# A decoder block on one core: x and the normed x turned by VectorE instead of TensorE in the front

## The chip, the core and the metric

The kernel runs on one core of one Trainium2 chip. The metric is the device time of one execution in microseconds, the median of several runs. TensorE's granted clock is 1.00 of its upper level in the part of the run that matters here.

## What is computed

One layer of a hybrid decoder block, 1024 tokens of width 1024, float32:

```
u   = RMSNorm(x)
P   = u @ W_in                     -> [B | C | h | q | k | v]
y_c = B * causal_dwconv3(C * h)
y_a = sliding-window attention (8 heads, 2 kv heads, window 128, QK-norm, ALiBi, sinks)
x   = x + concat(RMSNorm(y_c), RMSNorm(y_a)) @ W_out
xn  = RMSNorm(x)
x   = x + MoE(xn)                  (64 experts, top 8 of 4 groups, and one shared expert)
```

## The kernel before

Tokens lie in 8 tiles of 128 rows. The kernel has a front (the mixer, tile by tile, and the router's part of the MoE), a short middle in which the shared expert runs while the table of routed jobs is made, and a long stage of routed jobs. Each engine has its own program, written out by hand in order, and the engines meet only by semaphores. The front of every engine is the function `step(T, N, NN, B)`, called for T = tiles 0 to 6: T is the tile whose attention runs, N the next (its input projection runs), NN the one after (its x is made ready), B the one before (its residual, norm and routing run). Tile 7 (TL) has a tail of its own, and tile 6 (TB) is its B.

TensorE contracts over partitions, so every operand with tokens in partitions has to be turned before it is projected. Three things are turned in each step:

- `t_x(NN)` (L745): eight 128x128 transposes of x into PSUM `psT`. VectorE's `read_uT` (L1389) multiplies by the norm's weight and writes `uT`, of which there is one. `project` (L754) reads it. The scale 1/rms of a row is applied later, when ScalarE's `read_group` (L1111) copies a projected group out of PSUM.
- `t_xn(B)` (L833): eight transposes of the normed residual `xn` into `psT`. ScalarE's `read_xn` (L1182) copies them to `xnT`, which shares its memory with `yT`. `router` (L839) reads it, and SP stores it to DRAM.
- `t_y(T)` (L812): the mixer's output, likewise. It is not touched.

TensorE's step, in order: project(N, group 0), scores(T), project(N, 1), t_xn(B), project(N, 2), t_p(T) (turning the probabilities), part of project(N, 3), p_v(T), router(B), the rest of project(N, 3) and half of project(N, 4), t_y(T), the rest of project(N, 4), out_project(T, 0), t_qk(N), position(B), t_x(NN), out_project(T, 1).

VectorE's step, in order (L1602): x1_add(B) (residual add out of PSUM, L1512), xn_rms(B), xn_scale(B) (L1525), soft_a(T) (scores times scale plus bias, L1454), soft_b(T) (row maxima, L1465), u_mul(N) (C * h, L1397), conv(N) (L1401), o_norm(T) (L1477), y_attn_rms(T), route(B) (L1530), read_yT(T) (L1496), qk_norm(N), x_rms(NN), read_pos(B), read_uT(NN), conv_gate(N), slots(B), y_conv_rms(N).

What ties them: ScalarE's exps(T) wait for soft_b, t_p waits for the exps. On ScalarE read_group(N, 1), the h group, stands behind the exps, and u_mul waits for it. SP's `shift_u(N)` stores C * h to DRAM behind u_mul and reads it back shifted by one and by two rows; conv waits for that. o_norm scales p_v's result; ScalarE squares and scales y_attn, and t_y waits for both halves of y. read_yT(T) stands behind route(B) on VectorE, and out_project(T, 0) waits for it. x1_add waits for out_project(T, 1) of the step before. GpSimd computes the reciprocal roots, stores xn and the residual (`store`, L595), and then, from step 2 on, issues eight indirect DMAs (`scatter_slots`, L615). x is loaded by SP into one of three buffers `x_sb` (L388), which later holds the residual too; the load of NN waits for the store of B's residual.

In the routed stage VectorE turns the gathered rows with STREAM_TRANSPOSE (`turn_x`, L1645, 64 partitions x 512 elements, read with a step of 8 words) and the hidden activations (`turn_h`, L1667, 32 partitions x 64 elements, read in runs of 32 words). The instruction turns blocks of 32x32.

```
def t_xn(T):
    pe.wait_ge(s_xn_ready, (T.t + 1) * 3)
    for k in range(KT):
        i = nc.tensor.transpose(psT[:, k, :], xn.rearrange("t (p k) -> t k p", k=KT)[:, k], ident[:, :])
    i.then_inc(s_txn, 1)
```

Of the kernel before, what the change touches and what calls it, by code (L numbers as in the profile page):

```python
# [20 lines left out]
P = 128  # L21
# [5 lines left out]
class Tile:  # L27


    def __init__(self, t):  # L30
        self.t, self.par, self.buf, self.use = t, t % 2, (t + 1) % 3, t // 3 + 1
        self.rows = slice(t * P, (t + 1) * P)


def hymba_moe(nc, x, mix_norm_w, w_in, conv_w, q_norm_w, k_norm_w, sinks, conv_out_norm_w, attn_out_norm_w,
# [36 lines left out]
    with ExitStack() as ctx:  # L72
# [55 lines left out]
        x_sb = cut(3 * D).rearrange("p (b n) -> p b n", b=3)  # L128
# [3 lines left out]
        uT = cut(D).rearrange("p (k n) -> p k n", k=KT)  # L132
# [67 lines left out]
        xT_shared = [uT] + [area[:, o:o + D].rearrange("p (k n) -> p k n", k=KT) for o in (gates_at, gates_at + 2 * DC)] + \  # L200
# [103 lines left out]
        x_ld = [sem(f"x_ld{b}") for b in range(3)]  # L304
# [25 lines left out]
        TB, TL = tiles[-2:]  # L330

# [55 lines left out]
        def _(sp):  # L387
            def load_x(T):  # L388
                sp.dma_start(x_sb[:, T.buf], x2[T.rows, :]).then_inc(x_ld[T.buf], 16)
# [35 lines left out]
            def step(T, N, NN, B):  # L425
# [114 lines left out]
        def _(pool):  # L540
# [54 lines left out]
            def store(T):  # L595
# [5 lines left out]
                pool.dma_start(x1_dram[T.rows, :], x_sb[:, T.buf]).then_inc(x1_st[T.par], 16)  # L601
# [139 lines left out]
        def _(pe):  # L741
# [3 lines left out]
            def t_x(T):  # L745

                pe.wait_ge(x_ld[T.buf], T.use * 16)
                if T.t == 1:
                    pe.wait_ge(s_uT_ready, 1)
                for k in range(KT):  # L750
                    i = nc.tensor.transpose(psT[:, k, :], x_sb[:, T.buf, k * P:(k + 1) * P], ident[:, :])  # L751
                i.then_inc(s_tx, 1)

            def project(T, g, ks=range(KT)):  # L754
# [8 lines left out]
                for k in ks:  # L763
                    i = mm(psP[:, bank, 0:n], uT[:, k, :], w_in_sb[:, k, c0:c0 + n], k == 0, k == KT - 1)
# [47 lines left out]
            def t_y(T):  # L812
                pe.wait_ge(s_yc_scaled, T.t + 1)
                pe.wait_ge(s_ya_scaled, T.t + 1)
                if T.t:
                    pe.wait_ge(s_xnT_ready, T.t)
                else:
                    pe.wait_ge(s_uT_ready, 2)
# [33 lines left out]
            def step(T, N, NN, B):  # L852
# [14 lines left out]
                if B:  # L867
                    t_xn(B)
# [23 lines left out]
                if NN:  # L892
                    t_x(NN)
# [96 lines left out]
            t_x(tiles[0])  # L990
# [3 lines left out]
            t_x(tiles[1])  # L994
# [109 lines left out]
        def _(act):  # L1104
            A = nc.scalar.activation

            def x_square(T):
                act.wait_ge(x_ld[T.buf], T.use * 16)
                A(junk[:, :], x_sb[:, T.buf], ACT.Square, accum_out=st_x[:, 0:1]).then_inc(s_x_sq, 1)
# [68 lines left out]
            def x1_square(T):  # L1178
                act.wait_ge(s_x1_ready, T.t + 1)
                A(junk[:, :], x_sb[:, T.buf], ACT.Square, accum_out=st_n[:, 0:1]).then_inc(s_x1_sq, 1)  # L1180

            def read_xn(T):  # L1182
                act.wait_ge(s_txn, T.t + 1)
# [8 lines left out]
            def step(T, N, NN, B):  # L1192
# [12 lines left out]
                if B:  # L1205
                    read_xn(B)
# [137 lines left out]
        def _(dve):  # L1344
# [44 lines left out]
            def read_uT(T):  # L1389

                dve.wait_ge(s_tx, T.t + 1)
                if T.t:
                    dve.wait_ge(s_proj, T.t * NGR)
                V.tensor_tensor(uT, psT[:, :, :], bc(mixw[:, :].unsqueeze(2), [P, KT, P]), ALU.mult) \
                 .then_inc(s_uT_ready, 1)
# [120 lines left out]

            def xn_rms(T):

                dve.wait_ge(s_x1_sq, T.t + 1)
                if T.t:  # L1520
                    dve.wait_ge(s_txn, T.t)
# [360 lines left out]
```

## Time and profile before

| what | value |
|---|---|
| median of 3 runs | 1391.63 us (1389.9 to 1392.19) |
| the profiled execution | 1393.29 us, its span 1391.5 us |
| TensorE busy | 1364.0 us (98%) |
| VectorE busy | 942.7 us (68%) |
| ScalarE busy | 690.1 us (50%) |
| GpSimd busy | 562.7 us (40%) |
| the front (tiles 0 to 6 stepped) | 0 to 441.6 us |
| the middle | 441.6 to about 525 us |
| routed jobs and end | about 525 to 1391.5 us |

PE is TensorE, DVE VectorE, ACT ScalarE, POOL GpSimd, SP SyncE; L743 is the helper that issues every matmul. An instruction's row names what it writes and reads; `area` is the one large buffer in which most of the front's tiles lie, so rows are told apart by their line. "[5.53 <-PE ...]" at a row's end is the idle time of the engine before it and what ended it.

### The profile page before, as it was taken

To read this page: it belongs to the slowest core of one execution; us is meant where nothing else is said; L and a number is where in the kernel's file an instruction comes from. 1 tells how busy PE (TensorE), PEld (TensorE's weight loads), DVE (VectorE), ACT (ScalarE), POOL (GpSimd) and SP (SyncE) were. 2 spreads that over 40 slices of the span, in tenths; PEclk is the share of its full clock that TensorE was granted. 3 is DMA by queue.
4 is the path that set the end of the run, shared out by engine and by line. 5 is a ranking of instruction groups with operands and counts; after the bars stand their busy time and mean duration, and the time that the engine had idled before them with its cause. 6 is when DMAs were issued, how large, how long until landed. Compare 5 with 4: busy or idle time off the path is not lost.

```text
span 1391.5 us, 23960 instructions
## 1 busy us (share of the span) xinstructions
PE 1364.0 (98%) x5899; PEld 584.3 (42%) x5900; DVE 942.7 (68%) x2243; ACT 690.1 (50%) x646; POOL 562.7 (40%) x713
## 2 busy tenths in 40 slices
PE   7999999999999988999999999999999999999997
PEld 3456565565655542333333333333333333333333
DVE  2334443444535457888888888888888888888852
ACT  1223233233233311766666666666666666666640
POOL 3010303123031352555555555555555555555521
PEclk9999999999999999999999999999999999999999
DMA  9412112021116536999999999999999999999937
GB/s 343 188 61 84 46 38 84 13 72 46 38 69 283 190 123 222 347 355 315 354 332 379 322 322 356 288 300 276 318 317 375 368 350 329 332 321 299 373 49 215
DMA packets 76033, 330.10 MB, mean 237 GB/s; under 512 B 16008, under 2 KB 17545, under 8 KB 50325
## 3 DMA queue, kind: packets, MB, share of 16 engines
q1 hardware_dynamic: 45140, 249.62, 46.4%
q0 software_dynamic: 30848, 79.94, 23.3%
q8 instruction: 22, 0.36, 0.1%
q14 instruction: 23, 0.18, 0.0%
HBM read 282.74 MB, written 65.11 MB: 250 GB/s over the span
## 4 chain that ended last, share of the span: by engine, by line
PE 94%; DMA 3%; issue 1%; another core or an unknown queue 1%; ACT 0%; DVE 0%; SPq 0%; ACTq 0%; POOL 0%; POOLq 0%; DVEq 0%
PE psP L743 59%; PE psW L743 32%; DMA area<-x_dram 2%; PE psW L794 1%; DMA wts<-in_w_in_dram 1%; PE psT L820 1%; PE psT L836 1%; PE psT L751 0%; DMA area<-xn_dram,rows_i 0%; PE psW L771 0%; DVE bias L1651 0%; DMA x_dram<-area,sidx 0%; ACT wts L1261 0%; SPq L526 0%
## 5 line engine op out<-in xcount | busy, mean ns | idle before, releaser
L743 PE MATMUL psP<-wts,bias 128*64 (+1 forms) x1296 | 572.8, 595 | 7.9 <-DVE bias L1651 4.9
L743 PE MATMUL psP<-area,bias 128*64 128x512 f32 x1264 | 558.1, 594 | 0.0
L743 PE MATMUL psW<-wts,area 128*64 (+2 forms) x1592 | 426.6, 592 | 1.5 <-ACT wts L1261 0.9
L1651 DVE STREAM_TRANSPOSE bias<-area 64x512 f32<-64x512 f32 x316 | 352.3, 1115 | 8.1 <-DMA area<-xn_dram,rows_i 2.5
L743 PEld LDWEIGHTS psP<-wts,bias 128*64 128x64 f32 (+1 forms) x1296 | 179.4, 139 | 371.8 <-issue 371.8
L1672 DVE STREAM_TRANSPOSE area<-dsq 32x64 f32<-32x64 f32 x1264 | 298.4, 236 | 22.4
L743 PE MATMUL psP<-wts,area 128*128 128x512 f32 (+1 forms) x704 | 288.3, 561 | 5.6 <-DMA wts<-in_w_in_dram 4.3
L1268 ACT ACTIVATE area<-wts 128x4096 f32 x77 | 278.6, 3618 | 16.1 <-DMA wts<-in_w_exp_up_dram 6.6
L743 PEld LDWEIGHTS psW<-wts,area 128*64 128x64 f32 (+1 forms) x1592 | 153.1, 147 | 247.3 <-issue 245.8
L674 POOL DMA_INDIRECT area<-xn_dram,gidx x150 | 156.3, 1042 | 93.0 <-POOL gidx L670 65.3
L1251 ACT ACTIVATE area<-psW 128x1024 f32<-128x1024 f32 x79 | 80.9, 1024 | 226.9 <-PE psW L743 150.4
L743 PEld LDWEIGHTS psP<-wts,area 128*128 128x128 f32 x704 | 131.3, 192 | 136.7 <-issue 128.3
L698 POOL DMA_INDIRECT out_dram<-area,sidx x79 | 117.3, 1485 | 152.8 <-ACT area L1251 118.0
L743 PEld LDWEIGHTS psP<-area,bias 128*64 128x64 f32 x1264 | 173.6, 138 | 0.0
L1261 ACT ACTIVATE wts<-wts 128x2048 f32 x79 | 150.9, 1911 | 37.3 <-issue 35.6
L698 POOL DMA_INDIRECT x_dram<-area,sidx x79 | 112.5, 1424 | 25.4 <-issue 24.5
L1662 DVE SCALAR_TENSOR_TENSOR dsq<-dsq,area,psP 128x256 f32<-128x256 f32 x79 | 53.1, 672 | 84.8 <-ACT dsq L1235 82.8
L555 POOL TENSOR_TENSOR st_y<-st_y,minus_half 128x1 f32<-128x1 f32 x16 | 8.9, 557 | 180.7 <-DVE st_y L1349 180.7
L1132 ACT ACTIVATE area<-psP,st_x 128x512 f32<-128x512 f32 x32 | 21.8, 683 | 100.7 <-PE psP L743 95.8
L624 POOL DMA_INDIRECT slot_table<-pay,slot_i x64 | 62.6, 978 | 20.1 <-issue 19.1
L670 POOL COPY gidx<-rows_i 128x2 int32 x75 | 14.1, 188 | 123.5 <-DVE bias L1651 123.3
L1235 ACT ACTIVATE dsq<-psP 128x256 f32<-128x256 f32 x87 | 32.0, 368 | 55.2 <-PE psP L743 39.6
(225 smaller groups left out, 743.9 us busy)
## 6 DMA issues: line engine op xcount, KB each, us to landing
wts<-in_w_exp_gate_dram SPq DMA_DIRECT2D x64, 1024.0 KB
wts<-in_w_exp_up_dram SPq DMA_DIRECT2D x64, 1024.0 KB
wts<-in_w_exp_down_dram SPq DMA_DIRECT2D x64, 1024.0 KB
wts<-in_w_in_dram SPq DMA_DIRECT2D x4, 2048.0 KB, 17.4
area<-in_x_dram SPq DMA_DIRECT2D x8, 512.0 KB
wts<-in_w_out_dram SPq DMA_DIRECT2D x1, 4096.0 KB, 18.3
area<-u_dram SPq DMA_DIRECT2D x16, 256.0 KB, 2.9
xn_dram<-area POOLq DMA_DIRECT2D x16, 256.0 KB
```

The source lines that it names most:

```text
L624: pool.indirect_dma_start(out=table[:, :], out_offset=bass.IndirectOffsetOnAxis(ap=slot_i[:, n:n + 1], axis=0), in_=pay[:, t, j, :], in_of ...
L674: pool.indirect_dma_start(out=xg[:, par, g], out_offset=None, in_=xn_halves, in_offset=bass.IndirectOffsetOnAxis(ap=gidx[:, 2 * par + g:2 ...
L698: pool.indirect_dma_start(out=(out2, x1_dram)[b][:, :], out_offset=bass.IndirectOffsetOnAxis(ap=sidx[b][:, par:par + 1], axis=0), in_=ysb[ ...
L743: return nc.tensor.matmul(out_, lhsT, rhs, start=start, stop=stop)
L1132: A(dst, psP[:, bank, 0:n], ACT.Copy, scale=st_x[:, 2:3]).then_inc(s_proj_out, 1)
L1235: A(sg, psP[:, par, 0:FE], ACT.Silu).then_inc(s_silu, 1)
L1251: A(ysb[:, par], psW[:, 2:4, :].rearrange("p a n -> p (a n)"), ACT.Copy).then_inc(s_y_ready, 1)
L1261: A(dn_b, wts[:, bass.ds((e % NSLOT) * SLOTW + 2 * GUW, FT * D)], ACT.Copy).then_inc(s_dn_copy, 1)
L1268: A(gu_b[par].rearrange("p m k f -> p (m k f)"), wts[:, bass.ds((e % NSLOT) * SLOTW, 2 * GUW)], ACT.Copy) \
L1651: i = V.transpose(xT[par][u * HB:(u + 1) * HB, :, b * HB:(b + 1) * HB] .rearrange("p k (g t) -> p g k t", g=2), rows[:, u])
L1662: V.scalar_tensor_tensor(out=hh.rearrange("t (f p) -> t p f", f=FT), in0=sg.rearrange("t (p f) -> t p f", f=FT), scalar=w, in1=psP[:, par, ...
L1672: i = V.transpose(hT[1 - par][q * QUAD:(q + 1) * QUAD, :, t * QUAD:(t + 1) * QUAD], hh[t * QUAD:(t + 1) * QUAD].rearrange("t (f q p) -> t ...
```

## The change

x and the normed x are turned by VectorE, in 16 STREAM_TRANSPOSEs of 32 partitions x 256 elements each (`turn_x(NN)`, in two halves around u_mul; `turn_xn(B)`, behind xn_scale). x of tile 0 and the normed x of tiles 6 and 7 stay with TensorE. `turn_x` writes `uT` of the tile's parity, and `scale_uT` multiplies it in place. x comes into one buffer `x_in`; the residual has its own, `x_res`, loaded by a second DMA (tile 7's residual stays in `x_in`). ScalarE's read_xn goes from the step. The old `turn_x` of the routed stage is only renamed.

```diff
-        x_sb = cut(3 * D).rearrange("p (b n) -> p b n", b=3)
+        x_in, x_res = cut(D), cut(D)
+        uT_odd = cut(D).rearrange("p (k n) -> p k n", k=KT)
...
+        uT = [uT_even, uT_odd]
...
@@ SP
+            sp.wait_ge(s_tx, 1)
+            sp.wait_ge(s_x_sq, 1)
             load_x(tiles[1])
             sp.dma_start(w_out_sb, w_out[0].rearrange("(k p) n -> p k n", p=P)).then_inc(s_wout_ld, 16)
-            load_x(tiles[2])
+            load_residual(tiles[0])
...
-                if B and NN:
+                if NN:
+                    sp.wait_ge(s_tx, N.t + 1)
+                    sp.wait_ge(s_x_sq, N.t + 1)
+                    load_x(NN)
+                if B:
                     sp.wait_ge(x1_st[B.par], (B.t // 2 + 1) * 16)
                     sp.wait_ge(s_xn_ready, T.t * 3)
-                    load_x(NN)
+                    load_residual(T)
...
@@ TensorE, step
-                if B:
-                    t_xn(B)
...
-                if NN:
-                    t_x(NN)
...
-            t_x(tiles[1])
...
@@ ScalarE, step
-                if B:
-                    read_xn(B)
...
@@ VectorE
+            def turn_x(T, part=range(P // QUAD)):
+
+                if 0 in part:
+                    dve.wait_ge(s_x_ld, (T.t + 1) * 16)
+                    if T.t >= 2:
+                        dve.wait_ge(s_proj, (T.t - 1) * NGR)
+                for a in part:
+                    rows = x_in[a * QUAD:(a + 1) * QUAD].rearrange("t (k p) -> t k p", k=KT)
+                    for q in range(P // QUAD):
+                        i = V.transpose(uT[T.par][q * QUAD:(q + 1) * QUAD, :, a * QUAD:(a + 1) * QUAD],
+                                        rows[:, :, q * QUAD:(q + 1) * QUAD])
+                if P // QUAD - 1 in part:
+                    i.then_inc(s_tx, 1)
...
+            def turn_xn(T):
+                dve.wait_ge(s_xn_ready, T.t * 3 + 3)
+                for a in range(P // QUAD):
+                    rows = xn[a * QUAD:(a + 1) * QUAD].rearrange("t (p k) -> t k p", k=KT)
+                    for q in range(P // QUAD):
+                        i = V.transpose(xnT[q * QUAD:(q + 1) * QUAD, :, a * QUAD:(a + 1) * QUAD],
+                                        rows[:, :, q * QUAD:(q + 1) * QUAD])
+                i.then_inc(s_xnT_ready, 1)
...
                     xn_scale(B)
+                    turn_xn(B)
                 soft_a(T, first)
                 soft_b(T, first)
+                if NN:
+                    turn_x(NN, range(0, 2))
                 if N:
                     u_mul(N)
+                if NN:
+                    turn_x(NN, range(2, 4))
+                if N:
                     conv(N)
...
                 if NN:
-                    read_uT(NN)
+                    scale_uT(NN)
```

## Rows read from the trace of the kernel before

**Rows 1.** The page's chain that ended last, shares by engine.
```profile
PE 94%; DMA 3%; issue 1%; another core or an unknown queue 1%; ACT 0%; DVE 0%; SPq 0%; ACTq 0%; POOL 0%; POOLq 0%; DVEq 0%
```

**Rows 2.** The chain in time order, one step; columns: start us, us, what.
```profile
270.66 6.87 PE psP L743 x16
277.53 1.99 PE psW L743 x32
...
286.58 0.89 PE psT L836 x8
...
294.33 1.75 PE psW L794 x16
...
312.64 6.87 PE psW L743 x16
...
320.14 0.91 PE psT L751 x8
```

**Rows 3.** Busy time by stretch: PE, PEld, DVE, ACT, POOL, clock, DMA share, GB/s.
```profile
98.90:441.60 342.70, 342.70 (x1434) 199.08 (x1433) 153.02 (x370) 110.06 (x231) 76.22 (x87) 1.00 0.20 65
```

**Rows 4.** VectorE's groups by shape, whole run: busy us, mean ns, idle before.
```profile
L1651 DVE STREAM_TRANSPOSE bias<-area 64x512 f32<-64x512 f32 x316 | 352.3, 1115 | 8.1 <-DMA area<-xn_dram,rows_i 2.5
L1672 DVE STREAM_TRANSPOSE area<-dsq 32x64 f32<-32x64 f32 x1264 | 298.4, 236 | 22.4
L1662 DVE SCALAR_TENSOR_TENSOR dsq<-dsq,area,psP 128x256 f32<-128x256 f32 x79 | 53.1, 672 | 84.8 <-ACT dsq L1235 82.8 <-issue 1.8
...
L1380 DVE SCALAR_TENSOR_TENSOR bias<-area 128x256 f32<-128x256 f32 x8 | 2.8, 418 | 0.0
...
L1774 DVE TENSOR_SCALAR ring_i<-psW 128x102 int32<-128x102 f32 x1 | 0.3, 252 | 0.0
...
L1691 DVE CAST area<-psW 64x102 int32<-64x102 f32 x1 | 0.2, 245 | 0.0
```

**Rows 5.** The timeline of the same step, VectorE, and one row of ScalarE.
```profile
270.70 1.23 DVE L1514 TENSOR_TENSOR area<-psW,area 128x1024 f32<-128x1024 f32 x1 [2.60 <-PE psW L743]
...
273.96 1.28 DVE L1527 SCALAR_TENSOR_TENSOR area<-area,st_n,ffnw 128x1024 f32<-128x1024 f32 x1 [0.67 <-POOL st_n L555]
280.77 2.29 DVE L1460 SCALAR_TENSOR_TENSOR area<-psW,bias 128x2048 f32<-128x2048 f32 x1 [5.53 <-PE psW L743]
...
289.85 0.19 ACT L1147 ACTIVATE st_s<-st_s 128x8 f32<-128x8 f32 x1
290.65 0.69 DVE L1399 TENSOR_TENSOR area<-area 128x512 f32<-128x512 f32 x1 [4.78 <-ACT area L1132]
297.36 0.69 DVE L1406 TENSOR_TENSOR area<-area,convw 128x512 f32<-128x512 f32 x1 [6.02 <-DMA area<-u_dram]
...
302.27 0.69 DVE L1488 TENSOR_TENSOR area<-psW,st_s 128x512 f32<-128x512 f32 x1 [1.13 <-PE psW L743]
...
305.29 0.23 DVE L1542 TENSOR_TENSOR bi<-sc,rbias 128x64 f32<-128x64 f32 x1 [1.38 <-ACT sc L1190]
...
310.95 1.22 DVE L1501 TENSOR_TENSOR area<-psT,outw 128x1024 f32<-128x1024 f32 x1 [0.67 <-PE psT L820]
```

**Rows 6.** The timeline of GpSimd, same step: the third indirect DMA.
```profile
280.62 0.96 POOL L624 DMA_INDIRECT slot_table<-pay,slot_i  x1 [0.30 <-issue]
```

**Rows 7.** The timeline of the routed stage: a turn beside an indirect DMA.
```profile
803.62 4.51 DVE L1651 STREAM_TRANSPOSE bias<-area 64x512 f32<-64x512 f32 x4
803.70 1.49 POOL L698 DMA_INDIRECT out_dram<-area,sidx  x1 [1.66 <-ACT area L1251]
```

**Rows 8.** The timeline of the start and of step 0.
```profile
47.21 5.39 PE L743 MATMUL psP<-wts,area 128*128 128x512 f32 x12 [1.36 <-issue]
...
65.75 0.68 DVE L1399 TENSOR_TENSOR area<-area 128x512 f32<-128x512 f32 x1
...
76.89 0.69 DVE L1488 TENSOR_TENSOR area<-psW,st_s 128x512 f32<-128x512 f32 x1 [0.81 <-PE psW L743]
...
80.98 1.04 PE L820 MATMUL psT<-ident,area 128*128 128x128 f32 x8
```

More of the change, by code:

```diff
@@ L303, in hymba_moe @@
         s_x_sq = sem("x_sq")
-        x_ld = [sem(f"x_ld{b}") for b in range(3)]
+        s_x_ld = sem("x_ld")
+        s_res_ld = sem("res_ld")
         g_ld = [sem(f"g_ld{b}") for b in range(2)]
@@ L330, in hymba_moe, with residual @@
         TB, TL = tiles[-2:]
+        def residual(T):
+            return x_in if T is TL else x_res
         def side(j):
@@ L388, in load_x, with load_residual @@
             def load_x(T):
-                sp.dma_start(x_sb[:, T.buf], x2[T.rows, :]).then_inc(x_ld[T.buf], 16)
+                sp.dma_start(x_in, x2[T.rows, :]).then_inc(s_x_ld, 16)
+            def load_residual(T):
+                sp.dma_start(x_res, x2[T.rows, :]).then_inc(s_res_ld, 16)
             load_x(tiles[0])
@@ L600, in store @@
                                    xn.rearrange("t (u h n) -> t h u n", u=2, h=2)[:, h]).then_inc(s_xn_st, 16)
-                pool.dma_start(x1_dram[T.rows, :], x_sb[:, T.buf]).then_inc(x1_st[T.par], 16)
+                pool.dma_start(x1_dram[T.rows, :], residual(T)).then_inc(x1_st[T.par], 16)
             def rsqrt_qk(T):
@@ L743, in mm, with t_x_first @@
                 return nc.tensor.matmul(out_, lhsT, rhs, start=start, stop=stop)
[L745 to L749, printed above, removed]
+            def t_x_first():
+                pe.wait_ge(s_x_ld, 16)
                 for k in range(KT):
-                    i = nc.tensor.transpose(psT[:, k, :], x_sb[:, T.buf, k * P:(k + 1) * P], ident[:, :])
+                    i = nc.tensor.transpose(psT[:, k, :], x_in[:, k * P:(k + 1) * P], ident[:, :])
                 i.then_inc(s_tx, 1)
@@ L989, in _ @@
             pe.wait_ge(s_const_pool, 3)
-            t_x(tiles[0])
+            t_x_first()
             for g in range(NGR):
@@ L1520, in xn_rms @@
                 if T.t:
-                    dve.wait_ge(s_txn, T.t)
+                    if T is TL:
+                        dve.wait_ge(s_txn, 1)
+                    else:
+                        dve.wait_ge(s_xnT_ready, T.t)
                     dve.wait_ge(s_xn_st, T.t * 32)
@@ L1526, in xn_scale @@
                 dve.wait_ge(s_xn_ready, T.t * 3 + 2)
-                V.scalar_tensor_tensor(out=xn, in0=x_sb[:, T.buf], scalar=st_n[:, 2:3], in1=ffnw[:, :], op0=ALU.mult,
+                V.scalar_tensor_tensor(out=xn, in0=residual(T), scalar=st_n[:, 2:3], in1=ffnw[:, :], op0=ALU.mult,
                                        op1=ALU.mult).then_inc(s_xn_ready, 1)
+            def turn_xn(T):
[6 more added lines that the diff above has]
+                i.then_inc(s_xnT_ready, 1)
             def route(T):
@@ L1634, in _ @@
             dve.wait_ge(s_mixw_ld, 16)
-            read_uT(tiles[0])
+            scale_uT(tiles[0])
             constants()
             u_mul(tiles[0])
-            read_uT(tiles[1])
+            turn_x(tiles[1])
+            scale_uT(tiles[1])
             qk_norm(tiles[0])
@@ L1643, in _, with turn_rows @@
             y_conv_rms(tiles[0])
-            def turn_x(j, par, nth):
+            def turn_rows(j, par, nth):
                 dve.wait_ge(g_ld[par], nth * 32)
@@ L1801, in _ @@
             read_shared(2, side(2))
-            turn_x(NSH, 0, 1)
+            turn_rows(NSH, 0, 1)
             read_shared(3, side(3))
-            turn_x(NSH + 1, 1, 1)
+            turn_rows(NSH + 1, 1, 1)
             dve.wait_ge(s_xn_st, 32 * NT)
@@ L1809, in _ @@
             turn_h(NSH, 0)
-            turn_x(NSH + 2, 0, 2)
+            turn_rows(NSH + 2, 0, 2)
             h_mul(NSH + 1, 1, tab_w[:, 1:2])
             turn_h(NSH + 1, 1)
-            turn_x(NSH + 3, 1, 2)
+            turn_rows(NSH + 3, 1, 2)
             def jobs(i, ks):
@@ L1819, in jobs @@
                     turn_h(r + NSH, k)
-                    turn_x(r + (NSH + 2), k, i + 3)
+                    turn_rows(r + (NSH + 2), k, i + 3)
             one = routed_jobs(dve, 2, jobs)
```

41 lines of the change are left out of this document (20 added, 21 removed).

## The prediction

> **What bounds the kernel now.** I read the chain of waits first. It gives TensorE 94% of the span [rows 1]. That is an average over three stages, so the stage that the edit touches has to be read by itself: the front, eight tiles of mixer, up to 441.6 us. In time order its chain is TensorE alone and repeats [rows 2]: the project of the next tile starts at 270.66 and one step later at 320.14 + 0.91 + 6.87 = 327.92, so a step is 57.25 us, and nothing in it is a wait. The table by stretch says the same: in 98.90 to 441.60 TensorE is busy 342.70 of 342.70 us at granted clock 1.00, VectorE 153.02 [rows 3]. These are steps 1 to 6, five of 57.25 us and a last of 342.7 - 286.25 = 56.45. VectorE has over half of its time free. Free time isn't slack, though: it works in a fixed order, and what counts is how late each of its results may come.
>
> **What is removed.** From TensorE, in each of steps 1 to 6, the eight transposes of the normed x, 0.89 us [rows 2], and in each of steps 0 to 5 those of x, 0.91 us [rows 2]; also tile 1's ahead of step 0. If all else stayed hidden, steps 1 to 6 would save 6 x 0.89 + 5 x 0.91 = 9.9 us, and step 0 and the start up to 3.1 us (two turns and the 1.36 us in which TensorE waited for the scaling of tile 1 [rows 8]): 13 us. ScalarE loses the copy of the turned xn.
>
> **What is added: the price of a turn on VectorE.** Each is 16 STREAM_TRANSPOSEs of 32 partitions x 256 elements. No row has that shape; two stand on either side [rows 4]: 32x64 at 236 ns, read in runs of 32 words, and 64x512 at 1115 ns, read with a step of 8 words. Turning x reads as the first does, turning xn (viewed as p k) as the second. Plain VectorE rows run at 1.04 ns an element (1.22 us for 1024, 0.69 for 512 [rows 5]); 256 elements take 418 ns [rows 4]. A fixed part of 236 - 64 x 1.04 = 169 ns follows. Then x costs 169 + 256 x 1.04 = 436 ns, and the stepped form has (1115 - 169)/512 = 1.85 ns an element, so xn costs 642 ns. With 17 ns between two (four of 1115 ns take 4.51 us, [rows 7]) a turn of x is 7.2 us and a turn of xn 10.5. That a scattered access doubles the rate is seen elsewhere: the h_mul, 256 elements, takes 672 ns against the 418 [rows 4]. If instead both transposes have one rate, (1115 - 236)/448 = 1.96 ns, both turns cost 10.0 us. With no fixed part at all, xn costs at least 16 x (557 + 17) = 9.2. I take 10.4 for xn and 7.2 for x, range 9.2 to 10.7 for xn.
> On the step of 8 words the Trainium skill (SBUF — State Buffer, the box on cachelines) says that accesses which leave a 16-byte line each time pay a penalty; a step of 32 bytes does. Rows 4 agree with that reading but don't isolate it.
>
> **Where it lies.** turn_xn(B) stands between xn_scale and soft_a. In the step of 270.66, x1_add starts at 270.70 and xn_scale ends at 275.24 [rows 5]; the scores are done at 279.52 (277.53 + 1.99), and soft_a starts at 280.77 [rows 2, 5]. A turn of 10.4 us starting at 275.28 ends at 285.7: soft_a is some 5 us later than now. Behind it everything on VectorE keeps its order, and the waits between are other engines' answers to it (the exps, ScalarE's read of group h, then u_mul, the round trip of u through DRAM, the conv). So I carry the chain from x1_add to the next x1_add:
> - x1_add to xn_scale's end: 275.24 - 270.70 = 4.54 [rows 5]
> - turn_xn: 10.4, and 0.04 of hand-over
> - soft_a to the conv's start: 297.36 - 280.77 = 16.59 [rows 5]. The two halves of turn_x go into its holes: 3.6 us into the 4.78 before u_mul, 3.6 into the 6.02 before the conv [rows 5]. They cost nothing; at 10.0 us a turn they would cost 0.3.
> - the conv and o_norm's small operations, to 301.14 (302.27 less the idle 1.13, which vanishes since p_v is long done): 3.8
> - the scaling of y_attn to route's start: 305.29 - 302.27 = 3.02 (ScalarE's square, table load, sigmoid); route: 310.28 - 305.29 = 4.99; read_yT behind it: 1.25 [rows 5]
> - out_project 6.87 twice, t_qk and position 0.63 (312.64 + 6.87 to 320.14), hand-overs 0.2: 14.55 [rows 2]
> Sum 48.75 + 10.4 = 59.15 us. TensorE's own work is now 57.25 - 1.80 = 55.45. The larger sets the step. The loop closes because t_p waits for the exps, 9.3 us after soft_a (softmax operations on VectorE and the exps, which end at 290.04 [rows 5]), and from t_p's start TensorE has 312.64 - 294.33 = 18.3 us of work to out_project [rows 2], which is ready 2.1 us before yT is. So I expect two stalls a step: about 1.5 us ahead of t_p and 2.1 ahead of out_project. Now there is neither.
> What follows read_yT on VectorE (qk_norm, read_pos, the scaling of uT, conv_gate, slots) now ends before x1_add and has the same 14.5 us: hidden.
>
> **GpSimd's scatters.** In the steps with scatters soft_a starts 1.25 us after the scores, just after the third DMA_INDIRECT (280.77 beside 280.62) [rows 5, 6]. In step 1, which has none, it follows at once. That delay is hidden today. Eight of them, 0.96 us and 0.30 ahead of each [rows 6], go on until about 17 us into the step, and soft_a is now ready at 15, among them: 0 to 1.3 us more in each of steps 2 to 6. I take the middle, 0.6. The transposes themselves run beside such DMAs unharmed: four of 64x512 in 4.51 us, with a DMA_INDIRECT of 1.49 us begun 0.08 us after the first [rows 7].
> The Trainium skill (SBUF — State Buffer, who interferes with whom) says that a VectorE instruction with at most one SBUF input doesn't contend with GpSimd. Rows 7 agree for transposes; soft_a, with one input in SBUF and one in PSUM, started late against that rule. By the rule those 3 us would be nil.
>
> **Start and step 0.** x of tile 1 is turned and scaled while TensorE projects tile 0, into its own buffer, so its turn on TensorE, about 0.9, and the wait of 1.36 go [rows 8]; t_qk of tile 0 still waits for a qk_norm that starts when kv is read, so I count 1.7 of the 2.3. In step 0 the first half of turn_x (3.6) stands ahead of u_mul, which ran at 65.75 right behind soft_b [rows 8]; it is pushed by 3.6, and conv, o_norm and t_y behind it. To spare are the 0.81 idle before o_norm and, from its start at 76.89 with the 3.0 us to y_attn's scaling, 1.1 before t_y (80.98) [rows 8]: 1.7 lost. Then 0.9 for the missing t_x. Net -0.9, good to 1.5 either way.
>
> **Other moved steps.** SP issues one more load a step (x and the residual copy, 512 KB each); DMA's share of that stretch is 0.20 [rows 3], and both are queued ahead of u's store, whose trigger comes later than before. load_x(NN) waits for ScalarE's square of the tile before, done in the step before, and is needed only behind soft_b. The store of xnT is ready earlier. After step 6 nothing changes but an offset.
>
> **Sum.** Steps 1 to 6 go from 342.7 to 6 x 59.15 = 354.9: +12.2; scatters 5 x 0.6 = +3.0; step 0 -0.9. In all +14.3 us. The profiled execution took 1393.29 us (span 1391.5), the median of the runs 1391.63; the difference set on the median gives 1405.9, say 1406. On the profiled one it would be 1407.6.
>
> **Rivals.**
> A. The chain is as I say, but a turn of xn costs 6.8 to 8.2 us. Break-even is at 6 x (48.75 + D) = 342.7 + 0.9, D = 8.5 us. If time went with all elements of an instruction, not with those of a partition, the two rows give 0.18 + 8192 x 28.6 ns/1024 = 0.41 us, D = 6.8, and the step 55.6: 6 x 55.6 - 342.7 - 0.9 = -10, 1382 us. If only the 64 partitions made the wide form slow, xn costs as x, 7.2 us: step 55.95, -8, 1384 us. Against it: 64x102 takes 245 ns and 128x102 252 [rows 4], so partitions don't count there. Chance 0.10, the side of faster.
> B. The turn is cheap enough to vanish, and the whole 13 us is had: 1379 us. It needs D under 6.7 us.
> The Trainium skill (VectorE: DVE Perf Modes, the three transpose paths) has 311 ns for 128x128 in bf16, on VectorE, and calls it the fastest for blocks of 32x32. By that figure, for another type and without the moves between quadrants, eight such would be an estimated 2.5 us, and case B would hold. Rows 4 speak against it: 16 of 32x64 with their gaps alone take 4.0 us. Chance 0.03.
> C. Near break-even: D about 8.5 to 8.7 or other work taking up the delay: within 0.2% (2.8 us, about what a measurement of this kernel can tell from no change). Chance 0.05.
> D. The transposes contend with the scatters. Both lie at 5 to 17 us of the step; if VectorE stood still in eight of them of 0.96 us, the step grows by up to 7 us, five times: +50, 1441 us. Rows 7 speak against it. Chance 0.03.
>
> **How the numbers follow.** Mine 0.79 (1395 to 1413: D 9.2 and no scatter delay is 6 x 57.95 - 342.7 - 0.9 = +4.1, 1395.7, or 1.5 less with the start; D 10.7 with 1.3 us each is +19.7, 1411, and some for restarts). The range 1394.5 to 1413 leaves out A, B, D and part of C, 0.2. Faster 0.13, same 0.05, slower 0.82.
>
> **What would show it.** In the changed profile: STREAM_TRANSPOSEs of 32x256 at about 0.64 us in turn_xn and 0.44 in turn_x; in rows 3's stretch TensorE busy about 94% (55.5 of 59.15), its idle time before t_p and before out_project released by ScalarE's exps and VectorE's read_yT; steps of 59 to 60 us; soft_a some 15 us after x1_add. If xn's transposes show under 0.52 us, I'm wrong in sign by that term. If they show 0.64 and steps are still 55.5 us, the chain behind soft_a has slack that I missed.

## The result, and the profile after

| | before | changed |
|---|---|---|
| median of the runs | 1390.95 us (1389.9 to 1392.19, 4 runs) | 1405.44 us (1402.22 to 1410.89, 4 runs) |
| the profiled execution, its span | 1393.29, 1391.5 us | 1410.89, 1409.1 us |
| start of step 1 | 98.94 us | 100.31 us |
| steps 1 to 6, x1_add to x1_add | 342.69 us | 359.84 us |
| from there to the end of the span | 949.9 us | 948.95 us |

The ratio is 1.0107, 95% interval 1.0092 to 1.0121: slower by 14.5 us of 1391. The profiled execution is the slowest of the changed kernel's four. The front carries the whole difference; what follows it takes what it took.

The page of the changed kernel, the chain's shares by engine and, under it, the engines' busy time ([rows 1] had PE 94%):

```profile
PE 71%; DVE 13%; DMA 7%; issue 3%; ACT 3%; SPq 2%; POOL 1%; another core or an unknown queue 0%; POOLq 0%; DVEq 0%; ACTq 0%
...
PE 1360.6 (97%) x5795; PEld 574.6 (41%) x5796; DVE 1049.6 (74%) x2451; ACT 684.0 (49%) x640; POOL 563.7 (40%) x713
```

TensorE is as busy as ever, and VectorE, at 74%, is still not the busiest engine. But the chain now runs through VectorE, a DMA and ScalarE. Busy time by stretch, in the columns of [rows 3]: the six steps together, four of them alone, and two short stretches:

```profile
100.31:460.15 359.84, 339.53 (x1345) 189.74 (x1344) 246.20 (x547) 103.57 (x225) 76.26 (x87) 0.99 0.21 70
...
100.31:159.20 58.89, 56.02 (x225) 31.44 (x224) 42.38 (x94) 16.45 (x37) 6.27 (x8) 1.00 0.17 59
159.20:221.06 61.86, 57.72 (x225) 32.01 (x224) 42.38 (x94) 17.62 (x38) 14.07 (x16) 0.97 0.18 56
280.04:339.11 59.07, 56.03 (x225) 31.44 (x224) 42.38 (x95) 17.63 (x38) 14.11 (x16) 1.00 0.19 59
398.20:460.10 61.90, 57.73 (x226) 31.98 (x225) 34.30 (x76) 16.58 (x36) 13.56 (x15) 0.97 0.39 136
...
206.50:209.00 2.50, 2.50 (x5) 0.88 (x4) 0.38 (x3) 0.00 (x0) 1.96 (x1) 0.62 0.01 3
...
443.70:447.00 3.30, 3.30 (x4) 1.32 (x5) 1.98 (x5) 0.00 (x0) 1.10 (x1) 0.54 1.04 431
```

A step is 59 us instead of 57.25, and TensorE works for 56.0 of them. Two of the six take 61.9 us, for two reasons that these rows keep apart. TensorE is busy 1.7 us longer in them (57.7 for 56.0): their mean clock is 0.97, and the two short rows show where, with 0.62 and 0.54. And it is idle 1.1 us longer (4.1 for 3.0): in both steps the reload of u, for which the conv waits, took over 4.4 us, and in the four others 3.15 to 3.44. Here is that of the first of the two, from the chain in order of time:

```profile
187.14 4.43 DMA area<-u_dram
```

The transposes by shape (busy us, mean ns, idle before):

```profile
L1558 DVE STREAM_TRANSPOSE area<-area 32x256 f32<-32x256 f32 x96 | 60.5, 631 | 1.4
...
L1407 DVE STREAM_TRANSPOSE area<-area 32x256 f32<-32x256 f32 x112 | 48.7, 435 | 9.1 <-DMA area<-in_x_dram 7.6
```

Both prices are within 2% of the forecast (642 and 436 ns). And the timeline of one step; it answers to [rows 5]. The changed kernel's chain runs through most of VectorE's rows in it, between soft_b and u_mul through ScalarE's exps, and ahead of the conv through the store and reload of u. Columns: start us, us, what, and the idle time before:

```profile
280.04 1.23 DVE L1534 TENSOR_TENSOR area<-psW,area 128x1024 f32<-128x1024 f32 x1 [2.54 <-PE psW L759]
283.31 1.28 DVE L1550 SCALAR_TENSOR_TENSOR area<-area,st_n,ffnw 128x1024 f32<-128x1024 f32 x1 [0.67 <-POOL st_n L571]
284.62 10.28 DVE L1558 STREAM_TRANSPOSE area<-area 32x256 f32<-32x256 f32 x16
294.94 2.29 DVE L1481 SCALAR_TENSOR_TENSOR area<-psW,bias 128x2048 f32<-128x2048 f32 x1
299.94 3.57 DVE L1407 STREAM_TRANSPOSE area<-area 32x256 f32<-32x256 f32 x8
304.26 1.97 PE L808 MATMUL psW<-ident,area 128*128 128x128 f32 x16 [1.48 <-ACT st_s L1158]
304.82 0.69 DVE L1420 TENSOR_TENSOR area<-area 128x512 f32<-128x512 f32 x1 [1.31 <-ACT area L1143]
305.54 3.59 DVE L1407 STREAM_TRANSPOSE area<-area 32x256 f32<-32x256 f32 x8
311.32 0.69 DVE L1427 TENSOR_TENSOR area<-area,convw 128x512 f32<-128x512 f32 x1 [2.19 <-DMA area<-u_dram]
315.15 0.69 DVE L1509 TENSOR_TENSOR area<-psW,st_s 128x512 f32<-128x512 f32 x1
318.17 0.23 DVE L1574 TENSOR_TENSOR bi<-sc,rbias 128x64 f32<-128x64 f32 x1 [1.38 <-ACT sc L1201]
323.08 1.22 DVE L1522 TENSOR_TENSOR area<-psT,outw 128x1024 f32<-128x1024 f32 x1
324.35 1.13 PE L759 MATMUL psW<-wts,area 128*128 128x512 f32 x2 [1.57 <-DVE area L1522]
```

soft_a (L1481) had 5.53 us of idle time ahead of it in [rows 5]; now it starts 0.04 us behind the last transpose. The distances behind it are those that the forecast carried over: the conv (L1427) 16.38 us behind soft_a (16.59 forecast), the scaling of y_attn (L1509) 3.83 us later (3.8), route (L1574) 3.02 (3.02), read_yT (L1522) 4.91 (4.99). TensorE waits in two places, 1.48 us for the exps and 1.57 us for read_yT.

### The profile page after: what moved, and what is told of

The parts are those of the page before. It is cut to its first block, busy times and chain, and to the rows that moved or that the text cites. A ratio compares the mean times of both kernels' runs of the same rounds, so it can differ in the third digit from the quotient of the medians.

```text
span 1409.1 us, 23968 instructions
## 1 busy us (share of the span) xinstructions
PE 1360.6 (97%) x5795; PEld 574.6 (41%) x5796; DVE 1049.6 (74%) x2451; ACT 684.0 (49%) x640; POOL 563.7 (40%) x713
## 4 chain that ended last, share of the span: by engine, by line
PE 71%; DVE 13%; DMA 7%; issue 3%; ACT 3%; SPq 2%; POOL 1%; another core or an unknown queue 0%; POOLq 0%; DVEq 0%; ACTq 0%
PE psP L759 42%; PE psW L759 28%; DVE area L1558 4%; DMA area<-u_dram 2%; DMA area<-x_dram 2%; ACT area L1156 2%; DMA u_dram<-eq 1%; DMA u_dram<-area 1%; DVE st_s L1491 1%; DVE area L1481 1%; DMA x_dram<-area,sidx 1%; DVE area L1550 1%; SPq L403 1%; DVE area L1534 1%; DVE area L1522 1%
## 5 line engine op out<-in xcount | busy, mean ns | idle before, releaser
L759 PE MATMUL psW<-wts,area 128*64 (+2 forms) x1592 | 431.0, 595 | 13.7 <-DVE area L1522 11.4
L1156 ACT ACTIVATE area<-area,st_s 128x256 f32<-128x256 f32 (+1 forms) x64 | 30.8, 485 | 73.9 <-DVE st_s L1496 73.9
L1558 DVE STREAM_TRANSPOSE area<-area 32x256 f32<-32x256 f32 x96 | 60.5, 631 | 1.4
```

The source lines that it names most:

```text
L759: return nc.tensor.matmul(out_, lhsT, rhs, start=start, stop=stop)
L1156: A(s_sb[:, h, a:2 * P], s_sb[:, h, a:2 * P], ACT.Exp, bias=st_s[:, 2, h:h + 1], accum_out=st_s[:, 4, h:h + 1]).then_inc(s_exps, 1)
L1558: i = V.transpose(xnT[q * QUAD:(q + 1) * QUAD, :, a * QUAD:(a + 1) * QUAD], rows[:, :, q * QUAD:(q + 1) * QUAD])
```

## The experiments

Each edit is against the changed kernel, unless said. Runs of one group were compared with the kernel before on one chip; its medians there were 1388.73 (e1, e2, e3, e5), 1388.42 (e4, e6, e7, e8) and 1390.11 us (e9, e10).

### Each half of the change alone

e1 gives the normed x back to TensorE and keeps turn_x:

```diff
                     xn_scale(B)
-                    turn_xn(B)
...
@@ TensorE, step
+                if B:
+                    t_xn(B)
...
@@ ScalarE, step
+                if B:
+                    read_xn(B)
```

> The normed x goes back to TensorE and ScalarE, x stays with VectorE. Chain theory (the turn of xn between xn_scale and soft_a is what lengthens the step): the chain through VectorE falls back to 48.8 us plus the wait for the scores, so TensorE bounds each of steps 1 to 6 again, at 57.25 - 0.91 = 56.3 us; with 0 to 1 us from step 0 about 5 us under the kernel before, 1386 us, and TensorE without idle time between 100 and 440 us. Load theory (any 7 to 10 us of transposes on VectorE late its results): x's turn costs as the other did, in proportion 7.2/10.3 of the 1.8 us a step, so about 58.5 us a step and 1398 us.

e2 gives x back to TensorE and keeps turn_xn:

```diff
@@ TensorE, step
+                if NN:
+                    t_x(NN)
                 out_project(T, 1)
@@ VectorE, step
-                if NN:
-                    turn_x(NN, range(0, 2))
...
-                if NN:
-                    turn_x(NN, range(2, 4))
```

> x goes back to TensorE, the normed x stays with VectorE. Chain theory: x's turn lay in holes and was free, so nothing is won on VectorE; and TensorE's turn of x lies ahead of the second out_project, which is part of the loop, so steps 1 to 5 grow from 59.05 to 59.95 us and step 6 stays at 59.05: about 4 us above the changed kernel where TensorE's clock is the same, 1405 to 1412 us. Load theory: VectorE has 7.2 us less in each step, so the step shrinks to 57.5 to 58 us and the whole to about 1396 us.

e1: median 1384.67 us, ratio 0.9969 (0.9958 to 0.998). e2: 1404.12 us, 1.0116 (1.0099 to 1.0133). One step of e1 by stretch (columns of [rows 3]), and soft_a in its timeline:

```profile
267.84:324.25 56.41, 56.41 (x233) 32.48 (x232) 32.50 (x78) 18.73 (x39) 14.07 (x16) 1.00 0.19 61
```
```profile
276.70 2.29 DVE L1483 SCALAR_TENSOR_TENSOR area<-psW,bias 128x2048 f32<-128x2048 f32 x1 [4.32 <-PE psW L759]
```

And a step of e2:

```profile
278.13:337.86 59.73, 56.84 (x233) 32.26 (x232) 35.60 (x78) 17.68 (x38) 14.11 (x16) 1.00 0.17 58
```

The two halves have opposite signs. turn_x, without turn_xn, is hidden, and TensorE gets 0.84 us a step back, all of it time (56.41 of 56.41 busy). turn_xn alone makes the step 2.5 us longer although it takes work from TensorE. e2's step is 0.7 us above the changed kernel's, not the expected 0.9: t_x lies between the halves of out_project, on the path. Its median is just under the 1405 to 1412 us expected; set against the kernel before, it is 1.2 us above the changed kernel's (1.0116 against 1.0107), less than either interval is wide.

### Is the path through turn_xn, at full price?

e3 adds 4 more of the 16 transposes in front of turn_xn, into an idle tile:

```diff
             def turn_xn(T):
                 dve.wait_ge(s_xn_ready, T.t * 3 + 3)
+                rows = xn[0:QUAD].rearrange("t (p k) -> t k p", k=KT)
+                dose = tabR[:, :, :].rearrange("p g (a n) -> p (g a) n", n=QUAD)
+                for q in range(P // QUAD):
+                    V.transpose(dose[q * QUAD:(q + 1) * QUAD], rows[:, :, q * QUAD:(q + 1) * QUAD])
```

> Four more transposes of 32x256 with the step of 8 words ahead of the 16 of turn_xn, into an idle tile: 4 x 0.643 = 2.57 us. Chain theory: they stand in the loop with their whole time, so each of steps 1 to 6 grows from 59.05 to 61.6 us, +15.4 us over the changed kernel, about 1421 us. If the loop had slack, or if TensorE or a DMA set the step, under +5 us.

Median 1413.89 us, ratio 1.0179 (1.0162 to 1.0196). The added four in the timeline, and a step by stretch:

```profile
288.51 2.56 DVE L1558 STREAM_TRANSPOSE tabR<-area 32x256 f32<-32x256 f32 x4
```
```profile
283.94:345.42 61.48, 57.44 (x225) 32.64 (x224) 44.98 (x99) 17.70 (x38) 14.07 (x16) 0.97 0.17 56
```

2.56 us more of transposes, and the steps are 61.48 to 61.52 us (one 62.51, one 61.84) where the changed kernel has 58.9 to 59.2: the dose is paid in every step. Set against the kernel before in each group, the median moved by 10 us (1.0179 against 1.0107) and not by the expected 15.4. Between profiled executions the front grew by 14.9 us over e9's, which has no fall of the clock; the typical execution of the changed kernel is some 4 us slower than e9's profiled one, for which see the clock below.

The mean clock of 0.97 in that row comes from here (TensorE's timeline of the same step, and one short stretch):

```profile
310.73 2.84 PE L808 MATMUL psW<-ident,area 128*128 128x128 f32 x16 [4.04 <-ACT st_s L1158]
```
```profile
310.94:313.94 3.00, 3.00 (x17) 2.75 (x16) 2.58 (x6) 1.22 (x3) 0.00 (x0) 0.62 0.23 87
```

The stop ahead of t_p has grown from 1.48 to 4.04 us, and the clock falls behind it in each of the six steps. Steps 2 to 5 pay nothing for it: the time is taken from the second stop, ahead of out_project, which is gone from this timeline (1.57 us in the changed kernel). Step 1, where the 16 transposes of t_p took 3.68 us instead of 1.97, is the one of 62.51 us and pays 1.0.

### Does the step of 8 words set the price?

e4 reads xn in runs of 32 words and loads the router's and the shared expert's weights in the order that fits (the routed experts gather xn from DRAM and are untouched):

```diff
                 for a in range(P // QUAD):
-                    rows = xn[a * QUAD:(a + 1) * QUAD].rearrange("t (p k) -> t k p", k=KT)
+                    rows = xn[a * QUAD:(a + 1) * QUAD].rearrange("t (k p) -> t k p", k=KT)
...
-            const(wr[:, :, :].rearrange("p k n -> p (k n)"), w_router[0].rearrange("(p k) n -> p (k n)", k=KT))
+            const(wr[:, :, :], w_router[0].rearrange("(k p) n -> p k n", k=KT))
```

> turn_xn reads runs of 32 words as turn_x does; the router's weight and the shared expert's gate and up weights are laid out to match, so that the same is computed. If the step of 8 words is what made the 16 transposes of xn cost 631 ns against 435, they take 435 ns, a turn 7.1 us, and the loop 48.75 + 7.1 = 55.9 us a step against TensorE's own 55.5: steps of 55.9, about 19 us under the changed kernel and 6 to 8 under the kernel before, 1382 us; the shared weights' loads in packets of 1 KB might give some of it back in the middle. If the difference comes from the tile or the place (a contention with GpSimd's stores), they stay at 630 ns and the step at 59.

Median 1380.85 us, ratio 0.9947 (0.9931 to 0.9962): faster than before. The group of transposes and a step of e4:

```profile
L1565 DVE STREAM_TRANSPOSE area<-area 32x256 f32<-32x256 f32 x96 | 41.8, 436 | 1.5
```
```profile
210.54:266.38 55.84, 55.80 (x225) 31.52 (x224) 39.36 (x95) 17.82 (x38) 14.10 (x16) 1.00 0.21 62
```

Same instruction, shape and place; only the read pattern differs, and it is 436 instead of 631 ns. The step falls by 3.2 us, and TensorE is busy for 55.80 of 55.84: this is rival A's case (a turn of 7.2 us, a step of 55.95, faster), made by the edit.

### Does the place set the price?

e5 leaves every transpose at its price and puts them into VectorE's idle time: half of turn_xn ahead of soft_a, half behind soft_b, three quarters of turn_x between u_mul and conv, the last behind qk_norm:

```diff
-                    turn_xn(B)
+                    turn_xn(B, range(0, 2))
                 soft_a(T, first)
                 soft_b(T, first)
-                if NN:
-                    turn_x(NN, range(0, 2))
+                if B:
+                    turn_xn(B, range(2, 4))
                 if N:
                     u_mul(N)
                 if NN:
-                    turn_x(NN, range(2, 4))
+                    turn_x(NN, range(0, 3))
...
                 if NN:
+                    turn_x(NN, range(3, 4))
                     x_rms(NN)
```

> The same instructions at other places: half of turn_xn (5.15 us) stays ahead of soft_a, where VectorE idled 5.5 us in the kernel before, the other half goes behind soft_b into the hole of 4.8 us ahead of u_mul; three quarters of turn_x (5.4 us) stand in the hole of 6.0 us ahead of the conv, the last quarter (1.8) behind qk_norm. Chain theory: the place and not the amount costs, so TensorE bounds again: steps of 55.4 to 55.6 us, step 0 about 2.5 us shorter than before, in all 10 to 13 us under the kernel before, about 1379 us. Load theory: VectorE's busy time is unchanged at 42 us a step, so the time stays near 1400 us.

Median 1375.21 us, ratio 0.9904 (0.9887 to 0.992). The page's chain, a step by stretch, and VectorE's timeline in it:

```profile
PE 96%; DMA 1%; issue 1%; POOL 1%; DVE 1%; ACT 0%; ACTq 0%; SPq 0%; POOLq 0%; DVEq 0%
```
```profile
263.07:318.60 55.53, 55.53 (x225) 31.61 (x224) 42.58 (x94) 17.82 (x38) 15.11 (x16) 1.00 0.19 62
```
```profile
267.64 5.13 DVE L1558 STREAM_TRANSPOSE area<-area 32x256 f32<-32x256 f32 x8
272.78 2.29 DVE L1481 SCALAR_TENSOR_TENSOR area<-psW,bias 128x2048 f32<-128x2048 f32 x1
277.90 5.17 DVE L1558 STREAM_TRANSPOSE area<-area 32x256 f32<-32x256 f32 x8
283.11 0.69 DVE L1420 TENSOR_TENSOR area<-area 128x512 f32<-128x512 f32 x1
283.71 5.36 DVE L1407 STREAM_TRANSPOSE area<-area 32x256 f32<-32x256 f32 x12
289.48 0.69 DVE L1427 TENSOR_TENSOR area<-area,convw 128x512 f32<-128x512 f32 x1 [0.41 <-DMA area<-u_dram]
...
310.02 1.79 DVE L1407 STREAM_TRANSPOSE area<-area 32x256 f32<-32x256 f32 x4
```

VectorE is as busy as in the changed kernel (42.58 against 42.38 us a step), TensorE never waits, and the step is 3.5 us shorter. soft_a starts 9.7 us into the step instead of 14.9. All six steps take 55.53 or 55.54 us, and step 1 starts at 96.46 instead of 98.94: the start gives 2.5 us where the forecast counted 0.9, and no part of turn_x stands ahead of u_mul in step 0. It beats both kernels: by 13.5 us the kernel before on the same chip, and by some 28 the changed one (0.9904 against 1.0107, each set against the kernel before).

e6 is e5 with e4's read order.

> The spread order and the reading in runs together. Chain theory: in the spread order TensorE alone sets the step (55.54 us), so 3 us less on VectorE win nothing: within 1 us of the spread kernel in the front, 1374 to 1377 us. If VectorE still had a part in it, the step falls under 55.5 us or the total by over 3 us.

Median 1377.06 us, ratio 0.9922 (0.9908 to 0.9936). Its steps are e5's, with 3 us less of VectorE's work in each:

```profile
262.96:318.50 55.54, 55.54 (x225) 31.60 (x224) 39.48 (x95) 17.82 (x38) 15.12 (x16) 1.00 0.19 62
```

Once nothing waits for VectorE, the cheaper transpose buys nothing. The median is 1.9 us above e5's (2.5 if each is set against the kernel before of its group; the two intervals overlap). The front is the same in both; from step 6's end to the first routed turn e6 takes 81.4 us and e5 80.0, e4 81.2 and e1 80.1. The two kernels with the other layout of the shared weights are the longer ones. That their smaller packets cause it was argued from these four numbers, not tried by itself.

e8 puts turn_xn behind soft_b in one piece:

```diff
-                    turn_xn(B)
                 soft_a(T, first)
                 soft_b(T, first)
+                if B:
+                    turn_xn(B)
```

> The whole turn of xn moves behind soft_b, ahead of the first half of turn_x. soft_a, the exps and t_p are no longer late, so if the stall ahead of t_p is what costs, the time falls to about the kernel before's. Chain theory: the way to yT is then soft_a at 10.1 us, soft_b's end at 15.2, 10.3 + 3.6 us of turns, u_mul at 29.0, the conv 6.7 later, yT 13.1 after its start at 48.9, plus 14.6: a step of 63.4 us where the changed kernel has 59.05, so six steps make +26 us over it, about 1430 us.

Median 1417.09 us, ratio 1.0216 (1.0196 to 1.0237). Two rows of its timeline and a step:

```profile
293.65 2.29 DVE L1481 SCALAR_TENSOR_TENSOR area<-psW,bias 128x2048 f32<-128x2048 f32 x1 [4.32 <-PE psW L759]
...
298.70 10.35 DVE L1558 STREAM_TRANSPOSE area<-area 32x256 f32<-32x256 f32 x16
```
```profile
222.69:284.79 62.10, 58.82 (x225) 33.51 (x224) 42.59 (x95) 17.73 (x38) 14.12 (x16) 0.95 0.17 56
```

soft_a is on time again, and it is the slowest kernel of all: 10.35 us and the half of turn_x now stand in one hole ahead of u_mul. So it is not soft_a that may not be late, but the path through u_mul. The expected 63.4 us a step was 1.3 too long, since I had counted a delay of soft_a by the scatters that did not come. Step 6, which has no turn_x, took 60.3 us; with both, the median is 13 us under the 1430 expected. One step (step 4) took 63.6 us: in it the 16 matmuls of out_project took 8.63 us, with a fall of the clock.

e10 only splits turn_xn as e5 does and leaves turn_x where the change has it:

```diff
-                    turn_xn(B)
+                    turn_xn(B, range(0, 2))
                 soft_a(T, first)
                 soft_b(T, first)
+                if B:
+                    turn_xn(B, range(2, 4))
```

> Only turn_xn is split around the softmax; both halves of turn_x stay where the change has them. soft_a is on time again (9.8 us into the step), but ahead of u_mul now stand 5.15 + 3.6 us where the hole is 4.8. Chain theory: u_mul at 23.7, the conv at 30.4, yT at 43.4, and 14.6 more: 58.0 us a step, so three quarters of the loss stay (6 x 1.05 = 6 us under the changed kernel, 1393 to 1400 us). If being late with soft_a was what costs, the step falls to 55.5 to 56 us as in the spread kernel.

Median 1400.55 us, ratio 1.0085 (1.0061 to 1.0109), just above the 1393 to 1400 expected. Four steps by stretch, step 1 (no scatters), steps 3 and 4 (scatters), step 6 (no turn_x):

```profile
97.78:155.73 57.95, 55.80 (x225) 31.52 (x224) 42.49 (x94) 16.43 (x37) 6.26 (x8) 1.00 0.17 60
...
217.54:276.53 58.99, 55.99 (x225) 31.44 (x224) 42.61 (x95) 17.71 (x38) 14.10 (x16) 1.00 0.19 59
276.53:337.27 60.74, 57.69 (x225) 32.03 (x224) 42.56 (x94) 17.71 (x38) 14.07 (x16) 0.97 0.17 57
...
396.44:451.98 55.54, 55.54 (x225) 31.60 (x224) 34.51 (x77) 16.79 (x36) 13.52 (x15) 1.00 0.42 152
```

Splitting turn_xn alone recovers little: 5.17 us of it and 3.57 of turn_x share the hole ahead of u_mul. Step 6 has no turn_x and is at TensorE's own 55.54. So e5's gain needs both moves: with turn_xn split and turn_x in its old place the step is still 58 to 59 us (e10), and with turn_xn in one piece it is 59.7 us even when VectorE has no turn_x at all (e2). In the steps with scatters soft_a started 1.88 us behind the scores instead of 0.91, and step 3 is 1.04 us longer than step 1.

Steps 3 and 4 also give the price of a fall of the clock by itself. TensorE's out_project in the two:

```profile
261.77 7.13 PE L759 MATMUL psW<-wts,area 128*128 128x512 f32 x16 [2.71 <-DVE area L1522]
...
320.82 8.83 PE L759 MATMUL psW<-wts,area 128*128 128x512 f32 x16 [2.71 <-DVE area L1522]
```

The stop ahead is 2.71 us in both; behind it the clock fell in step 4 and not in step 3, and step 4 is 1.75 us longer. Step 2 had a fall and a reload of u of 4.48 us, and took 61.81; step 5 had a stop of 2.71 us and no fall, and took 59.17.

### The scatters

e7 changes the kernel before: GpSimd's scatters go behind its reciprocal root for y_attn.

```diff
-                if T.t >= 2:
-                    scatter_slots(T.t - 2)
                 rsqrt_ya(T)
+                if T.t >= 2:
+                    scatter_slots(T.t - 2)
```

> The kernel before with GpSimd's eight scatters of a step behind rsqrt_ya instead of ahead of it. If a scatter under way is what made soft_a start 1.25 us after the scores, it now follows them within 0.1 us in every step. If the delay has another cause (it came with the steps that have scatters, but also with the routing's results), it stays at 1.25. The time is that of the kernel before in either case (within 2 us): the delay was hidden; only the last scatters, later by some 20 us in the step, could hold up the middle.

Median 1388.17 us, ratio 0.9999 (0.999 to 1.0008). soft_a in a step with scatters:

```profile
164.86 2.29 DVE L1460 SCALAR_TENSOR_TENSOR area<-psW,bias 128x2048 f32<-128x2048 f32 x1 [4.32 <-PE psW L743]
```

It starts 0.04 us behind the scores in every step, where the kernel before has 1.18 to 1.31 in the steps with scatters. So the scatters do delay it there, at no cost in time. But e1 has the scatters at the same distance from the scores (the four nearest at -1.54, -0.20, 1.11 and 2.37 us), and its soft_a isn't late, as its row above shows (4.32 us of idle, none beyond the scores); nor is it in e8 or e5. e5 and e10 are alike up to soft_a, with the transposes, the scores and the scatters at the same times in the step within 0.03 us, and only e10's is late (by 0.99 us; its trace names nothing of this core that ended the wait). What decides it stays open.

### The changed kernel again

e9 is the changed kernel unaltered, beside e10.

> The changed kernel once more, unaltered. In its first profile steps 2 and 6 took 61.9 us where the four others took 59.0, and each held a stretch in which TensorE's granted clock was down to its lower level behind a wait; step 0 held one too. If these come and go, this profile has another number of long steps (each 2.9 us), the others stay at 58.9 to 59.2 us, and the run's time and mean clock go together: about 1400 us without any. If they belong to the program, the same three steps are long again.

Median 1403.98 us (1400.2 to 1407.17), ratio 1.0108 (1.0088 to 1.0127). Its profiled execution took 1400.2 us. Two steps by stretch:

```profile
158.08:217.96 59.88, 56.02 (x225) 31.44 (x224) 42.40 (x94) 17.60 (x38) 14.07 (x16) 1.00 0.18 58
...
277.17:336.12 58.95, 56.03 (x225) 31.44 (x224) 42.39 (x95) 17.64 (x38) 14.11 (x16) 1.00 0.18 59
```

Its six steps are 59.03, 59.88, 59.21, 58.95, 58.89 and 58.81 us, 354.8 in all, none at a mean clock under 1.00. The one of 59.88 us is step 2, with a reload of u of 4.15 us (3.13 to 3.50 in the others). Tile 2's out_project and tile 6's in TensorE's timeline of the changed kernel's profiled execution, then tile 2's in e9:

```profile
204.61 8.83 PE L759 MATMUL psW<-wts,area 128*128 128x512 f32 x16 [2.65 <-DVE area L1522]
...
443.70 8.83 PE L759 MATMUL psW<-wts,area 128*128 128x512 f32 x16 [2.70 <-DVE area L1522]
```
```profile
203.21 7.13 PE L759 MATMUL psW<-wts,area 128*128 128x512 f32 x16 [2.36 <-DVE area L1522]
```

## Why the prediction was right, and where it wasn't

1406.0 was forecast, 1405.44 came; the changed kernel run again gave 1403.98. Point by point:

**The price of a turn**: 631 and 435 ns against 642 and 436 forecast, a turn of xn 10.28 us against 10.4. Which of the readings behind it holds, e4 shows: the step of 8 words raises the rate, and without it a transpose of 32x256 takes the fixed part and 1.04 ns for each element of a partition, as the plain rows do. With the forecast's fixed part of 169 ns that is (631 - 169)/256 = 1.80 ns an element against (436 - 169)/256 = 1.04. Rivals A and B fall by these rows. So does the estimate of 2.5 us a turn, worked out from the 311 ns of the Trainium skill (VectorE: DVE Perf Modes, the three transpose paths). The Trainium skill (SBUF — State Buffer, the box on cachelines) puts a penalty on accesses that cross to a new 16-byte line each time; e4 agrees, with 631 ns at a step of 32 bytes against 436 in runs, but no run here tries a step within a line.

**The chain and the step**: 59.15 us by the sum, 58.8 to 59.2 measured in five of e9's six steps. The six took 354.8 us, against the forecast 354.9. Each piece agreed within 0.25 us, and e3 shows that turn_xn is on the path with all of its price. TensorE's own work, 55.45 forecast, is 55.53 where it never stops (e5) and 56.03 in the changed kernel, where the instructions behind a stop take a little longer (7.13 us for the first out_project, 7.03 for it in the kernel before); the stall ahead of out_project, 2.1 forecast, is 1.57 us. The break-even price of a turn, 8.5 us, has a measured one on each side: 7.2 in e4 (faster), 10.3 (slower). That turn_x costs nothing holds with this placement of turn_xn; in e10 its first half costs time, since the hole before u_mul is then taken.

**GpSimd's scatters: this term was wrong.** I put 3.0 us on a soft_a ready among them. In the changed kernel it starts 0.04 us behind the last transpose in every step, with scatters and without. The delay exists (e7 removes it from the kernel before, e10 pays 1.0 us a step for it), but I carried it over from one phase to another without a row for the new one. Rival D, in which the transposes contend with the scatters, is out: 631 ns each beside them. The rule of the Trainium skill (SBUF — State Buffer, who interferes with whom), by which the 3 us would be nil, gave the right term for the changed kernel. It does not explain the late soft_a of the kernel before and of e10; there the start is late, while the instruction itself takes 2.29 us as everywhere.

**Start and step 0**: -0.9 forecast; +0.1 in e9 and +1.4 in the profiled execution. The stall before t_y came as forecast in kind (1.85 and 2.00 us against 1.7), but what was counted as saved did not all come: in e9 TensorE reached its last project ahead of t_p 1.06 us earlier than in the kernel before (61.70 against 62.76), not 1.7. e5, with no transpose ahead of u_mul, has a start 2.5 us shorter than before.

**Not foreseen: the clock behind the stalls, and late reloads of u.** TensorE now stops twice a step, and in some executions its granted clock falls behind the stop: 0.62 over 206.5 to 209.0 us and 0.54 over 443.7 to 447.0, that is for a part of these stretches at the lower level, 1.2 GHz. Each time the 16 matmuls of out_project take 8.83 us instead of 7.13. That is 1.7 us of the 2.9 by which these steps exceed 59.0 (e10 has 1.75 for a fall at an unchanged stop); the other 1.1 to 1.2 us are the late reload of u, which e9's step 2 has without a fall (59.88 us). The forecast had neither. A third fall, in step 0, follows the 2.00 us ahead of t_y. The stops before the other two were 2.65 and 2.70 us; in e9 one of 2.36 us and one of 1.85 had no fall behind them. But the length of the stop doesn't decide it alone: of e10's four stops of 2.71 or 2.72 us, two had a fall behind them and two had none, and one of 3.39 us in e8 had none either. A fall costs time only where the loop's path runs: five of e3's six, behind the stop ahead of t_p, were paid for by the second stall, which was there anyway. The other three executions of the changed kernel beside the profiled one have mean clocks of 0.996 and 0.997. So the profiled execution, with a mean of 0.993, has a front 17.15 + 1.4 us longer, e9's 12.1 + 0.1 us, and the median of 14.5 us lies between the two. The prediction's "some for restarts" at the range's top was all that I had for it.

So the sum of +14.3 beside the measured +14.5 is partly luck: 3.0 us that I put on the scatters did not come, and a start without its gain, clock falls and late reloads of u, none of them foreseen at that size, made up for about as much. How much of the median is falls and how much reloads is not shown, since only two executions were profiled. What is shown is the term that decides the sign: six steps longer by some 2 us each through turn_xn.

## What to carry to other kernels

An engine that is busy for 45% of a stage (VectorE in the front before: 153 of 342.7 us) can come to set its time at 68% (246 of 359.8) if one new block stands ahead of the instruction on which a chain of answers from other engines hangs. Write down the gaps of its timeline with what ends each, and cut the new work so that no piece is much longer than the gap that it goes into: the same 32 transposes a step cost 14 us with half of them in one piece ahead of soft_a and earned 13.5 us when spread (e5). Shortening the instruction by its read pattern (e4) did nearly as much a step (3.2 us against 3.5) while it was on the path, and nothing once it was in a gap (e6); try the place first.

## What the runs showed of the hardware

- A STREAM_TRANSPOSE of 32x256 float32 takes 435 ns read in runs of 32 words and 631 ns read with a step of 8 words; a full turn of 128x1024 as 16 of them takes 7.2 or 10.3 us on VectorE, where TensorE has 0.89 us for it and another engine a copy.
- Stops of 2.00, 2.65, 2.70 and 4.04 us in TensorE's stream were followed by the lower clock level, one of 2.36 us and those of 1.3 to 1.9 us in e9 were not, and stops of 2.71 and 2.72 us in e10 were in two cases out of four. Ahead of out_project a fall cost 1.7 us, on 16 matmuls of 128x512 float32.
- soft_a, which reads PSUM and SBUF, starts 1.0 to 1.3 us late beside GpSimd's indirect DMAs in the kernel before and in e10, and not in e1, e5 and e8, though in e1 and e5 it lies at the same distance from them. Transposes beside the same DMAs keep their 631 ns. The cause wasn't found.
- The store and reload of u through DRAM is part of the changed kernel's loop, so its variation is now seen. The reload took 4.43 and 4.53 us in steps 2 and 6 of the profiled execution and 4.15 in step 2 of e9, against 3.13 to 3.50 in the nine others, and each late one made its step about 1 us longer. What made them late was not found.
